# Input transposes by DMA into a second h^T buffer, eight PSUM banks and paired convolutions, in an eight-core hybrid conv/conformer block

## The reference

```python
def mixer_layer(x, c, ...):                          # x (B, L, 1024)
    shift, scale, gate = split(silu(c) @ w_ada + b_ada)     # per sequence
    h = rmsnorm(x, norm_g) * (1 + scale) + shift
    p = h @ w_in                                     # (B, L, 3584)
    a_in, a_b, a_c, a_z, b_v, b_g, b_z = split(p)    # 7 x 512 columns
    y_a = a_b * dwconv3(a_c * a_in) * silu(a_z)
    u = dwconv31(b_v * sigmoid(b_g)) + conv_b_b
    y_b = silu(head_layernorm(u, ln_g, ln_b)) * silu(b_z)   # 64 channels a head
    return x + gate * (concat(y_a, y_b) @ w_out)
out = rmsnorm(mixer_layer(x, c, ...), final_g)       # depth 1
```

## Time and profile before

| | |
|---|---|
| median of 3 runs | 2573.29 us (2569.99 to 2576.30) |
| the profiled execution, its own time | 2571.52 us |
| its span, slowest core | 2570.0 us |
| TensorE busy | 2428.4 us, 94% |
| VectorE, ScalarE, GpSimd busy | 48%, 48%, 30% |
| mean granted TensorE clock | 0.989 |

### The profile page before, as it was taken

The page is one execution under the profiler, slowest core; times in us unless marked ns, Lnnn a source line. Parts: engine busy times, 40 slices in busy tenths (PEclk is TensorE's granted clock), DMA queues, the critical chain, the costliest instruction groups (busy, mean ns, idle before and its releaser), DMA issues.

```text
span 2570.0 us, 46749 instructions; the slowest of 8 cores (2563.3 to 2570.0 us)
## 1 busy us (share of the span) xinstructions
PE 2428.4 (94%) x14724; PEld 1074.0 (42%) x14724; DVE 1245.8 (48%) x1972; ACT 1231.0 (48%) x2054; POOL 781.0 (30%) x838
## 2 busy tenths in 40 slices
PE   5799999999999999999999999999999999999995
PEld 1334444444444444444444444444444444444432
DVE  1234454545454545454545455455455455445455
ACT  1144555544555554455554455554454554455544
POOL 3113333223323223323323323323323323333314
PEclk9899999999999999999999999999999999999998
DMA  9954223344322344322334322344422334432232
GB/s 220 200 134 125 87 81 92 117 125 125 96 80 91 109 125 125 107 78 83 109 125 133 118 70 88 101 133 125 125 82 82 102 118 125 125 94 80 61 110 99
DMA packets 89914, 283.05 MB, mean 110 GB/s; under 512 B 15016, under 2 KB 24400, under 8 KB 89680
## 3 DMA queue, kind: packets, MB, share of 16 engines
q1 hardware_dynamic: 80176, 270.64, 35.0%
q0 software_dynamic: 9504, 9.44, 2.7%
HBM read 168.96 MB, written 67.13 MB: 92 GB/s over the span
## 4 chain that ended last, share of the span: by engine, by line
PE 70%; ACT 15%; issue 6%; POOL 3%; DMA 3%; DVE 2%; another core or an unknown queue 0%; ACTq 0%; SPq 0%; POOLq 0%; DVEq 0%
PE pb L446 50%; PE pb L646 12%; PE pb L575 6%; ACT L605 3%; ACT L609 3%; ACT tp L607 3%; POOL yT L619 2%; ACT tp L615 2%; DMA w_in_sb<-w_in 2%; PE pb L586 1%; ACT tp L608 1%; ACT gb L553 1%; ACT sq L580 1%; ACT tp L465 1%; DVE tp L563 0%
## 5 line engine op out<-in xcount | busy, mean ns | idle before, releaser
L446 PE MATMUL pb<-hT,w_in_sb 128*128 128x512 bf16 x7168 | 1594.7, 381 | 18.7 <-DMA w_in_sb<-w_in 16.7
L446 PEld LDWEIGHTS pb<-hT,w_in_sb 128*128 128x128 bf16 x7168 | 699.4, 98 | 860.8 <-issue 50.8
L646 PE MATMUL pb<-w_out_sb,yT 128*128 128x512 bf16 x2048 | 470.7, 380 | 17.4 <-POOL yT L619 16.6
L465 ACT ACTIVATE tp<-pb 128x512 f32<-128x512 f32 x384 | 225.1, 595 | 488.5 <-PE pb L446 487.8
L619 POOL TENSOR_TENSOR yT<-tp,gb 128x512 bf16<-128x512 f32 x128 | 145.1, 1155 | 862.1 <-ACT tp L615 862.1
L658 POOL TENSOR_TENSOR xb<-tp,xb 128x512 f32<-128x512 f32 x256 | 321.7, 1267 | 142.0 <-DVE tp L656 123.8
L693 ACT ACTIVATE tp<-xb 128x1024 bf16<-128x1024 f32 x128 | 135.3, 1057 | 428.9 <-POOL xb L658 428.9
L646 PEld LDWEIGHTS pb<-w_out_sb,yT 128*128 128x128 bf16 x2048 | 195.5, 98 | 247.6 <-issue 37.5
L703 DVE SCALAR_TENSOR_TENSOR xb<-xb,rsE,fg_bc 128x1024 f32<-128x1024 f32 x128 | 164.4, 1284 | 227.1 <-POOL rsE L701 227.1
L575 PE MATMUL pb<-V,WC 128*32 128x512 bf16 x4096 | 244.4, 381 | 0.0
L656 DVE TENSOR_TENSOR tp<-pb,gate_bc 128x512 f32<-128x512 f32 x256 | 173.7, 689 | 121.5 <-PE pb L646 109.8
(11 more groups left out here) (74 smaller groups left out, 1503.7 us busy)
## 6 DMA issues: line engine op xcount, KB each, us to landing
xb<-x SPq DMA_DIRECT2D x256, 512.0 KB, 6.4
y<-xb SPq DMA_DIRECT2D x128, 512.0 KB, 2.7
V<-u SPq DMA_DIRECT2D x128, 135.9 KB, 2.6
V<-u SPq DMA_DIRECT2D x128, 135.8 KB, 2.6
V<-u SPq DMA_DIRECT2D x128, 135.6 KB, 2.7
xb<-w_ada SPq DMA_DIRECT2D x24, 512.0 KB, 9.7
w_in_sb<-w_in POOLq DMA_DIRECT2D x14, 512.0 KB, 28.3
gate_bc<-gate_scratch SPq DMA_DIRECT2D x5, 512.0 KB, 7.2
```

The source lines that it names most:

```text
L446: T.op("tensor", lambda e, bank=bank, kc=kc: e.matmul(bank[:], lhsT=w_in_sb[:, kc, col0:col0 + 128], rhs=hT[:, kc, :], start=(kc == 0), st ...
L465: T.op("scalar", lambda e: e.activation(out=t[:], in_=bank[:], func=func, scale=scale), reads=[bkey], writes=[tkey])
L646: T.op("tensor", lambda e, kc=kc: e.matmul(bank[:], lhsT=yT[:, kc, sub * 128:(sub + 1) * 128], rhs=w_out_sb[:, kc, h * NT:(h + 1) * NT], s ...
```

## The change

The transposes leave TensorE. For each 128-row piece of `xs`, SP issues one DMA transpose into one of two `hT2` buffers (tile i uses buffer i % 2), and VectorE applies scale and shift in place (`a_mod`). They are issued for tile i+1 after `a1(i)`, behind `d_loads`; on VectorE's queue `a_mod` stands ahead of every `d_evac` of the same `stage_d`. Squares, root and scaling work on two row pieces at a time (`a_half`), and the x loads come in pairs, with `XB` cut to six buffers. All eight PSUM banks are one ring. `middle` runs the convolutions in two pairs, each with its own norm block, and `stage_d` leads with six groups over six rows of `yT`. At the start the `w_ada` pieces pass through four buffers that lie in `V`, the small loads go to ScalarE's queue, and the loads of tile 1, tile 2 and `fg` are held until certain pieces of `w_in` have landed.

```diff
         t1_sb = [sb("t1%d" % i, [128, 4, NT + 2], BF16) for i in range(2)]
@@ -221,13 +220,13 @@
         ssE = sb("ssE", [128, 8], F32)
         msE = sb("msE", [128, 8], F32)
         rsE = sb("rsE", [128, 8], F32)
-        XB = Ring("xb", [sb("xb%d" % i, [128, D], F32) for i in range(8)], T)
+        XB = Ring("xb", [sb("xb%d" % i, [128, D], F32) for i in range(6)], T)
+        Vf = V[:].rearrange("p g j t -> p (g j t)").bitcast(F32)
+        VS = Ring("vs", [Vf[:, i * D:(i + 1) * D] for i in range(4)], T)
         TP = Ring("tp", [sb("tp%d" % i, [128, NT], F32) for i in range(6)], T)
-        PB = Ring("pb", [ps("pb%d" % i, [128, NT], F32) for i in range(6)], T)
-        ptr_t = [ps("ptr%d" % i, [128, 2 * NT], BF16) for i in range(2)]
-        PTR = Ring("ptr", [ptr_t[0][:, 0:NT], ptr_t[1][:, 0:NT]], T)
-
-        cur = {"eidx": 0}
+        PB = Ring("pb", [ps("pb%d" % i, [128, NT], F32) for i in range(8)], T)
...
-        def a_load(i, after=()):
-            for sub in range(4):
+        def a_load(i, subs, after=()):
+            for sub in subs:
                 xbuf, xkey = XB.next(pin=True)
...
-        def a_scale():
-            T.op("vector", lambda e: e.tensor_scalar(out=msA[:], in0=ssA[:], scalar1=1.0 / D, scalar2=RMS_EPS, op0=ALU.mult, op1=ALU.add),
-                 reads=["ssA"], writes=["msA"])
-            T.op("gpsimd", lambda e: e.tensor_tensor(out=rsA[:], in0=msA[:], in1=mhalf[:], op=ALU.pow), reads=["msA", "mhalf"], writes=["rsA"])
-            for sub in range(4):
...
+        def a_scale(half):
+            c = slice(2 * half, 2 * half + 2)
...
-        def a_compute():
+        def a_half(half):
+            a_square(2 * half)
+            a_square(2 * half + 1)
+            a_scale(half)
+
+        def a_transpose(i):
+            b = i % 2
+            for kc in range(8):
+                T._need("sync", [T.lastw.get(("hT", b, kc))] + T.readers.get(("hT", b, kc), []))
             for sub in range(4):
-                a_square(sub)
-            a_scale()
-
-        def a_transpose(kc):
-            pt, pkey = PTR.next()
-            for sub in range(4):
-                T.op("tensor", lambda e, sub=sub: e.transpose(out=pt[:, sub * 128:(sub + 1) * 128],
-                                                              in_=xs[:, sub, kc * 128:(kc + 1) * 128], identity=ident[:]),
-                     reads=[("xs", sub), "ident"], writes=[pkey], signal=(sub == 3))
-            return pt, pkey
-
-        def a_T_group(i, kc):
-            s = tile_seq[i]
-            pt, pkey = a_transpose(kc)
-            T.op("vector", lambda e: e.tensor_scalar(out=hT[:, kc, :], in0=pt, scalar1=gsT[:, kc, s:s + 1],
+                T.dma("sync", lambda e, sub=sub: e.dma_start_transpose(out=hT2[b][:, :, sub * 128:(sub + 1) * 128], in_=xs[:, sub, :]),
+                      reads=[("xs", sub)], writes=[("hTr", b, sub)], semkey=("tr", b, sub))
+
+        def a_mod(i, kc):
+            s, b = tile_seq[i], i % 2
+            T.op("vector", lambda e: e.tensor_scalar(out=hT2[b][:, kc, :], in0=hT2[b][:, kc, :], scalar1=gsT[:, kc, s:s + 1],
                                                      scalar2=shT[:, kc, s:s + 1], op0=ALU.mult, op1=ALU.add),
-                 reads=[pkey, "gsT", "shT"], writes=[("hT", kc)])
-
-
-
-        def mod_load(kc, third, pin=False):
-            xbuf, xkey = XB.next(pin=pin)
-            T.dma("sync", lambda e: e.dma_start(out=xbuf[:], in_=wada_d[kc * 128:(kc + 1) * 128, third * D:(third + 1) * D]),
-                  writes=[xkey], semkey=("xl", xkey[1]))
+                 reads=["gsT", "shT"] + [("hTr", b, q) for q in range(4)], writes=[("hT", b, kc)])
...
-        a_load(0)
-        a_compute()
+        a_load(0, range(4))
+        a_half(0)
+        a_half(1)
+        a_transpose(0)
         order = [(blk, kh) for blk in (5, 4, 0, 2, 3, 1, 6) for kh in range(2)]
         mbank, mbkey = PB.next(pin=True)
         for kc in range(8):
             for third in (1, 0):
-                xbuf, xkey = mod_load(kc, third)
+                xbuf, xkey = mod_load(kc, third, VS)
...
-                    small_load(t, d, key)
+                    small_load(t, d, key, "scalar")
...
-        if ntiles > 1:
-            a_load(1, after=[("w_in", 2, 1)])
-        T.dma("sync", lambda e: e.dma_start(out=fg_bc[:], in_=fg_d.partition_broadcast(128)), writes=["fg_bc"], semkey="ld_fg")
+            a_mod(0, kc)
+        a_load(1, range(4), after=[("w_in", 3, 1)])
+        T.dma("sync", lambda e: e.dma_start(out=fg_bc[:], in_=fg_d.partition_broadcast(128)),
+              reads=[("w_in", 6, 1)], writes=["fg_bc"], semkey="ld_fg")
...
+        def ln_var(j):
+            cc, ckey, vv, vkey = cst[j]
+            vb, vbkey = PB.next(pin=True)
+            T.op("tensor", lambda e: e.matmul(vb[:], lhsT=Bm[:], rhs=vv[:], start=True, stop=True), reads=["Bm", vkey], writes=[vbkey])
+            sqr.unpin(vkey)
+            cst[j] = (cc, ckey, vb, vbkey)
+
...
-        def stage_d(i, nxt=None, mid=None, lead=4):
+        def stage_d(i, nxt=None, lead=6):
             banks = {}
 
             def d_mm(n, kcs):
@@ -662,23 +673,16 @@
                     d_square(xbuf, xkey, i * NT + sub * 128)
 
             def d_group(n):
-                d_mm(n, range(4, 8) if n in banks else range(8))
+                d_mm(n, range(6, 8) if n in banks else range(8))
                 d_evac(n)
                 if n in (5, 7):
                     d_finish()
 
-            d_mm(0, range(4))
-            d_mm(1, range(4))
-            for n in range(4):
-                if nxt is not None:
-                    a_T_group(nxt, 2 * n)
-                    a_T_group(nxt, 2 * n + 1)
-                if n == 0 and mid is not None:
-                    mid()
-                if n < 2:
-                    d_mm(2 + n, range(4))
-            for n in range(4, lead):
-                d_mm(n, range(4))
+            for n in range(lead):
+                d_mm(n, range(6))
+            if nxt is not None:
+                for kc in range(8):
+                    a_mod(nxt, kc)
             for n in range(8):
                 d_group(n)
...
         def middle(p, i):
             run([
-                "zb 2", "zb 3",
-                lambda: conv_a(p, 0), lambda: conv_b(0), "a2 0",
-                lambda: conv_a(p, 1), lambda: conv_b(1), lambda: conv_mean(0), "a2 1",
-                lambda: conv_a(p, 2), lambda: conv_b(2), lambda: conv_mean(1), "a2 2",
-                lambda: conv_a(p, 3), lambda: ln_pair(p, (0, 1)), lambda: conv_b(3), lambda: conv_mean(2), "a2 3",
-                lambda: conv_mean(3), "zb 0"], i)
-            held = ln_act((2, 3))
-            zb(i, 1)
-            stage_d(p, i + 1, mid=lambda: ln_fin(p, held))
+                "zb 2", lambda: conv_a(p, 0), "a2 0",
+                lambda: conv_b(0), lambda: conv_b(1), lambda: conv_mean(0), lambda: conv_a(p, 1), "zb 3",
+                lambda: conv_mean(1), lambda: ln_var(0), "a2z 1", lambda: ln_pair(p, (0, 1)), "a2b 1",
+                lambda: conv_b(2), lambda: conv_b(3), lambda: conv_a(p, 2), "a2 2",
+                lambda: conv_mean(2), lambda: conv_mean(3), lambda: conv_a(p, 3), "a2 3",
+                lambda: ln_pair(p, (2, 3)), "zb 0", "zb 1"], i)
+            stage_d(p, i + 1)
...
-        if ntiles > 1:
-            a_compute()
+        a_half(0)
+        a_half(1)
+        a_transpose(1)
         if ntiles > 2:
-            a_load(2)
+            a_load(2, (0, 1), after=[("w_in", 6, 1)])
         a2_all(0)
         for j in range(4):
             zb(0, j)
-        if ntiles > 1:
-            for kc in range(8):
-                a_T_group(1, kc)
-        for kc in range(4):
+        for kc in range(8):
+            a_mod(1, kc)
+        for kc in range(2):
             gate_load(kc)
...
                 if fin:
                     d_finish()
+                if nxt is not None and j == 1:
+                    a_half(0)
+                if nxt is not None and i > 1 and j == 3:
+                    a_load(nxt, (2, 3))
+            if i == 1:
+                gate_load(6)
+                gate_load(7)
...
-            while fin:
-                d_finish()
             v_fill(prev)
+            if nxt is not None and i == 1:
+                a_load(nxt, (2, 3))
...
-                if nxt is not None:
-                    a_square(j)
-            if nxt is not None:
-                a_scale()
+                if nxt is not None and j == 2:
+                    a_half(1)
             t1_halo(i)
             if i == 1:
                 d_loads(prev)
+            if nxt is not None:
+                a_transpose(nxt)
             if i + 2 < ntiles:
-                a_load(i + 2)
+                a_load(i + 2, (0, 1))
             if i < ntiles - 1:
                 middle(prev, i)
             else:
```

More of the change, by code:

```diff
@@ L209, in build_nc @@
         xs = sb("xs", [128, 4, D], BF16)
-        hT = sb("hT", [128, 8, NT], BF16)
+        hT2 = [sb("hT%d" % i, [128, 8, NT], BF16) for i in range(2)]
```

(48 more changed lines are left out.)

37 lines of the change are left out of this document (15 added, 22 removed).

## The result

The changed kernel takes 2469.08 us at the median of four executions, where the kernel before, beside it, takes 2572.39: a ratio of 0.957 [0.951, 0.963] (in brackets, here and below, the 95% interval). One of the four took 2888.72 with a granted clock of 0.81 on one die; such executions are left out of every ratio, and of the medians of the experiments, and the other three lie between 2448.78 and 2469.25. That is faster, as forecast, and 21 us above the 2448 that were forecast. The profiled execution took 2469.25.

A forecast was written before the change was run, and what follows sets the result against it. TensorE was taken to bound the kernel, with 70% of the chain, and DMA the start. From the profiled 2571.5 us, -135 for the steady tiles and +11 at the start gave 2447.5, say 2448 us; range 2420 to 2525.

The forecast's parts named there:

- The steady tile: Tiles 2 to 31: period falls from 76.65 to 72.0 us, a gain of 4.65, times 29 tiles: -135 us.
- the wait for `yT`: Output stage: last rows of `yT` are covered by 11.2 us of matmuls, with 0.9 us to spare.
- the 1.2 us in the convolutions: Time lost from first convolution to output stage, 0.75 in one mean matmul's wait for ScalarE; 0.6 was forecast to remain.
- the prediction's 3.96: Output stage: 17.77 us less 13.8 of matmuls, given to transposes and the wait for `yT`; all of it goes.
- The price and cover of a transpose: Each DMA transpose costs 0.87 to 7.5 us, 3 taken; four land by 47 us into the tile, due at 63.
- too long: Rival, chance 0.13: transposes run one after another at 9.7 us each, period 80.7, time 2770; decides from about 8 us each.
- The start: Before tile 1: first projection moves from 48.50 to about 64, tile 1 begins at 137 instead of 125.95, +11 us.
- cheap transposes: Rival, chance 0.16: transposes take 1.5 us or less, the start gains 5 instead of losing, time 2431.
- Tile 1: Tile 1, 87.07 us before: no gain counted, waits for the gate's pieces eat the 4.65; -5 to +10.
- the first x pair now adds 1.2 ahead of them: SP's queue: the pair adds 1.2 us ahead of `d_loads`, which end 26.3 us into the tile; transposes start moving at about 33.
- The mean matmuls: Convolutions: rival, chance 0.08, that each of four mean matmuls waits 0.75 us for ScalarE, tile keeps 3 us, time 2518.

## Why the prediction was right, and where it was off

**The steady tile** was right in kind and 0.44 short: 72.0 was forecast, an undisturbed tile is 71.56, a gain of 5.09 for 4.65. The output stage became 64 matmuls in a row and the wait for `yT` went, as argued. Of the 1.2 us in the convolutions I had let 0.6 stand; at the prices of the earlier trace rows the stretch of 24.54 us is the work itself, and none stands.

Where the 5.09 came from is not what the name of the change suggests. Back from 71.56: the transposes on TensorE add 1.47, the old order of the output stage 0.15, two banks in that order 0.92. That is half. The old order of the convolutions by itself adds 1.35 at its quietest tiles. These sum to 3.9. Where the other 1.2 lie is not shown: both old orders together were not run, nor were the two `hT2` buffers, the halves of `a_half` and the x pairs undone. So the prediction's 3.96 for the transposes and the wait for `yT` was right as the stage's sum, of which TensorE's own time for the transposes is 1.47.

**The price and cover of a transpose** were right: 1.6 to 2.0 us of the DMA engines, inside my 0.87 to 7.5 and under the 3 that I took, and free when doubled. VectorE waited for one only once, before tile 1 (12.48). The rival *too long* is out, and with it the estimate from the Trainium skill, "VectorE: DVE Perf Modes", section "The three transpose paths": at 1309 ns for 128x128 a transpose of eight such blocks would take 10.5 us, an estimate from that page of the Trainium skill; it lands in 5.5 and holds the engines for 2. The 390 ns that the Trainium skill has there for TensorE are far from the 1.47 us for 32 blocks here, 0.046 each in a stream of matmuls. The Trainium skill's 261 GB/s, "DMA: Bandwidth & Descriptors", section "Latency and other measured facts", are nearer: 262 KB in 1.6 to 2.0 us are 131 to 164 GB/s.

**The start** was mis-sized. The first projection came where it was forecast; tile 1 came at 122.61, not at 137. The rows show where the 14 us lie: `w_in` was released at 42.44 (49 forecast) and its first ten pieces took 41 us (47 forecast), so tile 1's x went out at 83.07 and not at 96. From there to the issue of its transposes pass 20 us (18 counted), and from that to its first projection 20 (23 counted). What I gave as the answer for cheap transposes (-5) is nearer than +11, but not for its reason: TensorE had done with tile 0 and waited 7.04 us for these transposes. **Tile 1** gained 8 us on this core where I counted none; which part of the change gave them was not tested.

**The step that failed** is the sentence on SP's queue: "the first x pair now adds 1.2 ahead of them", which is the second pair, ahead of the `d_loads`. I counted the issue time of the moved pair, not its megabyte of data, and asked only whether the transposes behind it would be in time, which had 16 us to spare, not the V copies between, which are wanted about 12 us after the first goes out (1766.68 to 1778.99 in the bad tile). I also took SP's times from the earlier trace rows, while the copies now go out 5 us later in the tile; whether `u` in time would have cured the wait as well, no run shows. That term was missing from the sum: 56 us on the slowest core, 14 to 56 by core.

The sum with the measured terms: 2571.5 - 29 x 5.09 - 3 - 8 = 2413, and 56 of lateness give 2469, the time measured. That my number was only 21 us off is thus luck, two errors against each other: about 35 us too little gain (13 steady, 14 start, 8 tile 1) and 56 us of an unseen wait.

**The mean matmuls** did not wait, as forecast: three such waits in the whole run.

## What to carry to other kernels

A load that is moved in a queue is to be costed by its data as well as by its issue, against every transfer behind it, and first against the one with the least time to spare, not against the one that the change is about. When work leaves the bounding engine, price its bare time, its pacing and the order around it apart: here the transposes' own time was 1.47 of 5.09 us. Take what a wait costs from the lengths of the tiles and not from the list of waits: here the list has 24.5 us and the tiles 56, a small part of it because the clock fell behind some waits.

## What the runs showed of the hardware that was not expected

A DMA transpose of 128 x 1024 bf16 from SBUF to SBUF holds SP for 1.2 us at the least and up to 9.8 (in a stretch with a DMA share of 1.08), and what stands behind it in SP's queue waits with it. It makes about a thousand packets, (214336 - 80176) / 128 = 1048 more per transpose, yet streams at 131 to 164 GB/s. Two loads of 512 KB directly ahead of them on the queue take copies of 136 KB from 2.5 to 5.7 us to land, with the copies issued at the same time in the tile. After a wait of under 3 us for `V` the granted clock was 0.59 for 8 us, although TensorE had been busy for 33 us before; after most of the shorter waits it stayed at 1.00.
